# Decoder layer in one kernel: three feed-forward products moved ahead of the stage change, and the down projection's additions and requests re-timed

## What is computed

```
def finish(x, o_att, y_ssd, W):
    mix = concat([o_att, y_ssd])
    h = x + mix @ W['w_out']
    u = rmsnorm(h, W['norm_ffn'])
    return h + (silu(u @ W['w_gate']) * (u @ W['w_up'])) @ W['w_down']
```

## Time and profile before

| what | us |
|---|---|
| median of three runs | 1787.85 |
| profiled execution | 1803.71 |
| its span | 1801.9 |
| TensorE busy (94% of the span) | 1693.7 |
| VectorE busy (64%) | 1153.6 |
| ScalarE busy (42%) | 762.5 |
| GpSimd busy (23%) | 407.9 |

### The profile page before, as it was taken

The page is one execution under the profiler, slowest core; times in us unless marked ns, Lnnn a source line. Parts: engine busy times, 40 slices in busy tenths (PEclk is TensorE's granted clock), DMA queues, the critical chain, the costliest instruction groups (busy, mean ns, idle before and its releaser), DMA issues. The chain is left out here.

```text
span 1801.9 us, 32859 instructions
## 1 busy us (share of the span) xinstructions
PE 1693.7 (94%) x11957; PEld 1436.6 (80%) x11957; DVE 1153.6 (64%) x2521; ACT 762.5 (42%) x1593; POOL 407.9 (23%) x488
## 2 busy tenths in 40 slices
PE   5999998999999989998888996999999999999998
PEld 5999997888876756555546876999999999877777
DVE  7632257766675645565354368877788877597875
ACT  6322462777672335455343234323223232364432
POOL 1321120766664643344432001000000000000000
PEclk9999999899998989999988998999999999999999
DMA  5633111121001256556683231322223321684333
GB/s 160 103 108 109 36 42 25 28 48 26 19 12 36 82 208 217 164 193 236 211 298 132 73 100 56 112 88 94 88 94 115 114 88 65 235 289 125 86 112 104
DMA packets 161031, 204.19 MB, mean 113 GB/s; under 512 B 55110, under 2 KB 109423, under 8 KB 160850
## 3 DMA queue, kind: packets, MB, share of 16 engines
q1 hardware_dynamic: 142170, 135.00, 24.8%
q0 software_dynamic: 18432, 67.12, 11.1%
q10 hardware_dynamic: 312, 0.52, 0.1%
HBM read 164.69 MB, written 37.90 MB: 112 GB/s over the span
## 5 line engine op out<-in xcount | busy, mean ns | idle before, releaser
L2911 PE MATMUL banks<-u_sum,w_sum 128*128 128x264 f32 x3696 | 450.7, 284 | 9.7 <-DVE w_sum L2944 9.7
L2911 PEld LDWEIGHTS banks<-u_sum,w_sum 128*128 128x128 f32 x3696 | 450.4, 189 | 9.9 <-issue 9.8
L470 PE MATMUL banks<-u_parts_mix,w_in_parts 128*128 128x352 f32 x1440 | 243.6, 326 | 4.4 <-DVE u_parts_mix L837 4.4
L470 PEld LDWEIGHTS banks<-u_parts_mix,w_in_parts 128*128 128x128 f32 x1440 | 230.7, 189 | 7.8 <-DVE u_parts_mix L837 4.8
L1979 PE MATMUL banks<-turned,cmp_w 128*128 128x512 f32 x256 | 133.7, 605 | 5.0 <-DVE turned L2106 3.0
L2104 ACT ACTIVATE turned<-banks 128x512 f32<-128x512 f32 (+1 forms) x136 | 78.6, 587 | 138.5 <-PE banks L1967 105.1
L3240 PE MATMUL banks<-wd_hi,gd_hi 128*128 128x512 f32 x308 | 122.3, 397 | 9.6 <-DVE y_sums L3289 7.6
L3240 PE MATMUL banks<-wd_lo,gd_hi 128*128 128x512 f32 x308 | 121.9, 396 | 0.0
L3240 PE MATMUL banks<-wd_hi,gd_lo 128*128 128x512 f32 x308 | 121.7, 395 | 0.0
L1967 PEld LDWEIGHTS banks<-consts,rows_grouped 128*128 128x128 f32 x512 | 65.0, 144 | 68.7 <-issue 57.1
L2834 ACT ACTIVATE w_sum<-w_whole 128x512 fp32r<-128x512 f32 x110 | 66.6, 624 | 105.9 <-DVE w_whole L2938 105.9
(11 more groups left out here) (436 smaller groups left out, 3127.5 us busy)
## 6 DMA issues: line engine op xcount, KB each, us to landing
gd_whole<-g_sums SPq DMA_DIRECT2D x77, 256.0 KB, 2.7
g_sums<-silu_gate SPq DMA_DIRECT2D x55, 256.0 KB, 2.1
w_gate_raw<-in_w_gate SPq DMA_DIRECT2D x11, 1024.0 KB, 5.4
w_up_raw<-in_w_up SPq DMA_DIRECT2D x11, 1024.0 KB, 5.3
w<-in_w_down SPq DMA_DIRECT2D x44, 256.0 KB, 5.2
w_in_raw<-in_w_in SPq DMA_DIRECT2D x29, 256.0 KB, 3.4
g_sums<-s SPq DMA_DIRECT2D x22, 256.0 KB, 2.3
x_tile<-in_x_prompt SPq DMA_DIRECT2D x8, 512.0 KB, 4.2
```

What stands on the lines that cost most here:

```text
L470: mm = nc.tensor.matmul(bank[:, 0:PIECE], w[:, pb, :], u[:, pa, k, tokens(p)], start=(k == 0 and (pa, pb) == TERMS[0]), stop=(k == KT - 1 ...
L2911: mm = nc.tensor.matmul(bank(tg, i), wp[side, p][:, a, k, :], m.u[tg, i, b][:, k, :], start=(k == 0 and (a, b) == TERMS[0]), stop=(k == kh ...
```

## The change

1. Gate products 1, 3 and 5 of the first pair and token group 0 (`FIRST`) are computed in `stage_finish_mixer`, between the transposes of tiles 7 and 8, into banks 6, 7 and 2. Their weight sums and splits are made by VectorE and ScalarE behind the splits of tile 6, ahead of tile 7's addition. The splits of token products 4 and 2 (two of the seven) move from tile 6 to tile 5.
2. Group 1's token sums 4 and 7 are made by GpSimd (`EARLY_POOL`) and sums 1 and 3 by VectorE (`EARLY_DVE`) at the end of the mixer; 7, 1 and 3 only for 232 of 264 columns. The missing 32 columns (tile 8) and sum 6 are done by VectorE in the feed-forward stage, which no longer uses GpSimd.
3. `stage_ffn` starts with product 4. Four more small writes (memset) raise the semaphores for the work already done. The pair loop of TensorE has its first pair written out. Banks are renumbered in both stages (0 with 6, 1 with 7).
4. In the down projection the additions come in front of step 3 of each of the last four products (before: 4, 5, 5, 5), and SyncE asks for one entry of `later` per step until step 15, then for two.

```diff
+                pe.wait_ge(s.h_ready, 2 * NT)
+                for p, i in enumerate(FIRST):
+                    pe.wait_ge(m.first_split, p + 1)
+                    pe.wait_ge(s.u_split, p + 1)
+                    for k in range(KT // 2):
+                        for a, b in TERMS:
+                            mm = nc.tensor.matmul(m.bank[FIRST_BANKS[i]][:, 0:QUARTER], m.first_wp[p][:, a, k, :], m.u[0, i, b][:, k, :],
...
+                    mm.then_inc(m.first_done, 1)
                 turn_h(n - 1)
...
+                pool.wait_ge(s.u_whole, 2 * (NT - 1))
+                pool.wait_ge(s.mixed, 2 * n)
+                early_sum(EARLY_POOL[0], slice(0, QUARTER))
+                pool.wait_ge(s.u_whole, 2 * NT)
+                pool.wait_ge(m.early_sum, 1)
+                early_sum(EARLY_POOL[1], slice(0, EARLY_COLS))
...
+                        if i == NT:
+                            early_sum(EARLY_DVE[0])
                         dve.wait_ge(s.h_root, i + 1)
...
+                        if i == NT:
+                            early_sum(EARLY_DVE[1])
...
-                        for p in {5: range(3), 6: range(3, 7)}.get(i, ()):
+                        for p in {5: range(5), 6: range(5, 7)}.get(i, ()):
...
+                        for p in {NT - 2: range(len(FIRST))}.get(i, ()):
+                            dve.wait_ge(m.gate_in, 16)
...
-POOL_SUMS = 3
+FIRST, FIRST_BANKS = PRODUCTS[:3], {1: 6, 3: 7, 5: 2}
+EARLY_POOL, EARLY_DVE, EARLY_COLS = (4, 7), (1, 3), NT * P - 3 * QUARTER
...
-D_ADDED_AT = {3: 2, 2: 3, 4: 4, 1: 5, 6: 5, 7: 5}
+D_ADDED_AT = {3: 2, 2: 3, 4: 3, 1: 3, 6: 3, 7: 3}
...
-                            plans = ([ul[:1], [us[0], ul[1]], [us[1], ul[2]], ul[3:4], ul[4:5]],
+                            plans = ([first[:2], first[2:] + us[:2] + ul[:1], [ul[1], us[2], us[3], ul[2]], ul[3:4], ul[4:5]],
...
-                for f in weights((None, 0), 0):
-                    f()
+                dve.wait_ge(m.first_done, len(FIRST))
...
+                first = [lambda f=f, p=p: f((None, 0), 0, p) for f, p in
+                         ((w_sum, 4), (w_lo, 3), (w_sum, 5), (w_sum, 6), (w_lo, 4), (w_lo, 5), (w_lo, 6))]
...
-        later += [top[q], w(0, 1, 2 * q), w(0, 1, 2 * q + 1)]
-    later += [w(0, 1, p) for p in range(8, PAIRS)] + bottom
+        later += [top[q], w(0, 1, q)]
+    later += [w(0, 1, p) for p in range(4, PAIRS)] + bottom
...
-        for what in later[:2]:
+        count = 1 if j < G_SLOTS + PAIRS - 1 else 2
+        for what in later[:count]:
             one_of(what)
-        later = later[2:]
+        later = later[count:]
```

More of the change, by code:

```diff
@@ L2441, in stage_finish_mixer @@
     m.gate_raw = nc.alloc_sbuf_tensor_at("w_gate_raw", [P, KT, 2 * P], F32, offset=m.mix_start + size)
-    m.gate_raw_end = m.mix_start + size + KT * 2 * P * 4
+    first = Region(nc, m.mix_start + size + KT * 2 * P * 4, m.end)
+    m.first_whole, m.first_wp = {}, {}
+    for p in range(len(FIRST)):
+        m.first_whole[p] = nc.alloc_sbuf_tensor_at(f"w_whole_first_{p}", [P, KT // 2, P], F32, offset=first.at + KT // 2 * P * 4)
+        m.first_wp[p] = first(f"w_sum_first_{p}", [P, 2, KT // 2, P], F32R)
+    m.first_end = first.at
     low = Region(nc, m.base_end + 17 * size, m.mix_start)
@@ L2578, in _, with early_sum @@
             def _(pool):
+                def early_sum(i, cols):
+                    _, a, b, op = next(u for u in U_SUMS if u[0] == i)
+                    nc.gpsimd.tensor_tensor(m.u_whole[1, i][:, :, cols], m.u_whole[1, a][:, :, cols], m.u_whole[1, b][:, :, cols],
+                                            op).then_inc(m.early_sum, 1)
                 for k in SPLIT_BY_POOL:
@@ L2714, in stage_ffn @@
     mid = Region(nc, m.u1_end, m.mix_start)
-    top = Region(nc, m.gate_raw_end, m.end)
+    top = Region(nc, m.first_end, m.end)
     up_raw = top("w_up_raw", [P, KT, 2 * P])
@@ L2755, in over_pairs @@
         turn((None, last), False)
[L2757 removed]
+    with stage(nc, "landed*2 w_sum w_hi w_split u_sum u_hi u_split m_done copied c_done silu_done g_ready "
                    "t_sum plain_stored s5_stored first_stored second_stored "
@@ L2856, in first_gate @@
                     u_hi(1)
-                    copy(t, 0, 0, 5)
-                    u_hi(2)
-                    u_hi(3)
                     copy(t, 0, 0, 2)
-                    for p in range(4, 7):
+                    for p in range(2, 7):
                         u_hi(p)
@@ L2891, in turn @@
                                 silu(t, tg)
-                for p in range(7):
+                act.wait_ge(m.early_sum, len(EARLY_POOL))
+                act.wait_ge(m.early_sum_dve, len(EARLY_DVE))
+                hi((None, 0), 0, 3)
+                copy((None, 0), 0, 0, 5)
+                for p in range(4, 7):
                     hi((None, 0), 0, p)
@@ L2914, in turn @@
                                 mm.then_inc(s.m_done, 1)
-                with pe.Fori(0, last) as t:
-                    turn(t)
-                turn(last)
+                turn((None, 0))
+                with pe.Fori(0, last - 1) as t:
+                    turn((t, 1))
+                turn((None, last))
                 down_tensor(nc, pe, s, d)
-            @block.gpsimd
-            def _(pool):
-                for k in range(POOL_SUMS):
-                    i, a, b, op = U_SUMS[k]
-                    nc.gpsimd.tensor_tensor(m.u_whole[1, i][:, :, :], m.u_whole[1, a][:, :, :], m.u_whole[1, b][:, :, :],
-                                            op).then_inc(s.u_sum_pool, 1)
             @block.vector
```

72 lines of the change are left out of this document (54 added, 18 removed).

## The result

The changed kernel takes **1777.56 us** (median of 6 runs, 1776.73 to 1780.38) beside 1787.83 of the kernel before in the same comparison (6 runs, 1785.83 to 1788.24): ratio 0.9947, 95% interval 0.9937 to 0.9957. The forecast was 1774, range 1768 to 1780.5. The time lies in the range; of the 14.0 us forecast 10.3 came.

A forecast was written before the change was run, and what follows sets the result against it. TensorE, busy for 94% of the span, was taken as the bound. Stage change 8.7 us plus down projection 5.3 (13.6 freed, 8.3 lost) made 14.0 off 1787.85: 1774 us, range 1768 to 1780.5.

The forecast's parts named there:

- Early matmuls and split weights in the mixer, cost 0: Mixer's end: 36 matmuls fit TensorE's 4.6 us idle before tile 8's transposes; the added work costs 0, at worst 1 us.
- Turn-taking at the mixer's end: Two-input SBUF steps of VectorE and GpSimd alternate, holding sum 1; the new stage begins 1.5 us later, 0.4 without this.
- the case that I named through the Trainium skill: Mixer's end: tile 8's scaling also waits if GpSimd's sum 7 ends after 1089.5; forecast had it ending at 1088.4.
- Stage change 8.7 us: Gate to up products: TensorE starts up at 1113.9, later weights cost some 0.5 more, against 1123.1 before; 8.7 us gained.
- Late additions, 5.2 + 3.3 us: Last products of the down projection: earlier additions remove 5.2 us of `y_sums` waits and 3.3 us of half speed.
- Opening, 5.1 us: Start of the down projection: one request per step lands blocks sooner, saving 1.0 + 2.4 and 1.7 of half speed.
- the forecast's own sign: Down projection: waits standing at its first two products would show the forecast wrong in that term.
- `rest_h` too late, 8.3 us: Down projection, step 27: `rest_h` is requested only after step 26; 6.5 us idle and 1.8 of half speed lost.
- `rest_h` in time: Rival: the request for `rest_h` causes no wait in the down projection; gain 22.3 us, 1765.6 us; chance 0.08.
- late weight blocks: Rival: in product 3 of the down projection nine steps wait some 2.5 us each; net 8 us slower, 1796; chance 0.04.
- the stage change gave more than half: Answers the rival that the stage change gives half: 4 us less gained, 1778 us; chance 0.08.
- of the opening's loss a quarter stayed: Answers the rival that the down projection's opening stays as it is: 5.1 us missing, 1779 us; chance 0.17.

The follow-up runs named there:

- products_behind: The changed kernel with the 36 early matmuls behind tile 8's transposes instead of ahead of them; 1802.7 us, ratio 0.9985 to the kernel before.
- down_only: The kernel before with only the changed kernel's down projection edits (addition table and request list); 1804.4 us, ratio 0.9998 to the kernel before.
- rest_two_steps: The changed kernel with the request for the last rows of h at step 30 instead of 32; 1783.1 us, ratio 0.9873 to the kernel before.
- gate_only: The changed kernel with the additions and request list of the kernel before, leaving only mixer and gate changes; 1796.0 us, ratio 0.9943 to the kernel before.
- stores_later: The changed kernel with product 3's four stores issued behind step 33's requests instead of step 31's; 1794.8 us, ratio 0.9930 to the kernel before.

## Why the prediction was right, and where it was off

Each term of the sum was found at the place where the forecast had it. That the terms, as traced, add up to the timed gain is in part luck, as the end of this section says.

- **Early matmuls and split weights in the mixer, cost 0: right.** From tile 6's to tile 7's transposes it is 12.0 us before and after. products_behind showed that their place is worth more than I had given it.
- **Turn-taking at the mixer's end: the mechanism right, the held step another.** I had sum 1 held to over 2 us and the new stage 1.5 us later. Its 3.26 us and VectorE's timeline show that GpSimd's second sum gave way to sum 1 and ended late, and that tile 8's scaling then waited behind it. I had GpSimd 0.5 us ahead with sum 7; in the trace the two began 0.13 us apart, so which step was held hung on tenths. That is the case that I named through the Trainium skill (page "SBUF — State Buffer", section "Who interferes with whom": a `tensor_scalar` can be held too) and then set aside, since I had sum 7 end in time. The trace agrees: 1.88 us beside sum 7, 0.74 without it. The stage began 1.1 us later, not 1.5.
- **Stage change 8.7 us: right, 8.56 against the trace of before, 7.7 against that of down_only.** The first up product came at 1113.8 on the clock of before's trace, forecast 1113.9 and 0.5 behind. The half speed behind the 3.06 us wait was absorbed: VectorE was the pace. In rest_two_steps it lasted 5.4 us in place of 3.3, and the first up product still came 30.1 us behind the mark. gate_only gives 8.55.
- **Late additions, 5.2 + 3.3 us: the waits right, the half speed a matter of chance.** All five waits went. Of six waits of 1.7 to 1.8 us in three traces three were followed by half speed, so the fair price was 5.2 and some 1.7.
- **Opening, 5.1 us: 3.7 came.** The wait in step 7 and the half speed went; of 2.40 us 1.35 was left in the changed kernel's trace (0 to 1.35 over the nine executions whose list starts the same). By the forecast's own sign, a wait left at the first two products, this term was wrong; what sets the rest of the wait stays open. Its 2.1 and 3.9 MB also leave out the load `rest`, 0.35 MB.
- **`rest_h` too late, 8.3 us: it is the step that failed in size, 10.6.** Place, cause and order of events came as forecast. The term used landing times from a quiet queue, but four stores of 256 KB issued just ahead filled the DMA engines (share 1.03 over the 2 us from the block's request, 0.52 in stores_later): 0.8 us in the block's request, 0.8 in the landing. Without them it was 6.83. (The forecast's own terms for this wait add up to 6.4, not 6.5.) Half speed behind it cost 2.0 us, in place of 1.8.

Together the terms make 8.6 + 5.2 + 3.3 + 3.7 - 10.6 = 10.2 us, and 10.8 was traced, 10.3 timed. They are read against one execution of the kernel before, which had its long half speed at the stage change and both stretches in the last products; with 7.7 and 1.7 for these two the sum is 7.7. The timed gain lies, by its interval, between 7.7 and 11.3 us. The rivals: `rest_h` in time is refuted; so are late weight blocks, since no wait in the trace ends with one; the stage change gave more than half; of the opening's loss a quarter stayed.

## What to carry to other kernels

When a list of requests is thinned out, work out for its last entry when it is now issued and when it is needed; here the last entry took back 10.6 of the 12.2 us that the same edit and its neighbour gave, and moving it by two steps brings nearly all of it. Price a landing behind whatever the same queue has issued just ahead, stores included. Independent matmuls put in a gap can be worth more than their duration: here 4.6 us of them cost 6.2 when they stood behind the gap, 2.3 of it through half speed.

## What the runs showed of the hardware

- Half speed behind a short stop is not certain, and neither is its length. In the down projection it came behind three of six waits of 1.69 to 1.81 us, behind three of three of 2.40 to 2.45, and behind none of 1.23 or less. Behind the same 3.06 us at the stage change it lasted 3.3 us from TensorE's restart in the changed kernel (to 1081.7) and 5.4 in rest_two_steps (to 1100.8); at the old stage change, behind 9.70 and 9.98 us, it lasted 5.2 and 3.1. The rows are of the changed kernel and of rest_two_steps, with all five busy shares:

```profile
1079.00:1080.00 1.00, 1.00 (x7) 1.00 (x6) 1.00 (x3) 0.32 (x1) 0.00 (x0) 0.50 1.07 381
1081.00:1082.00 1.00, 1.00 (x7) 1.00 (x7) 1.00 (x3) 0.00 (x0) 0.00 (x0) 0.64 0.23 74
```

```profile
1098.00:1099.00 1.00, 1.00 (x6) 1.00 (x6) 1.00 (x3) 0.00 (x0) 0.00 (x0) 0.50 0.25 79
1100.00:1101.00 1.00, 1.00 (x7) 1.00 (x7) 0.61 (x1) 1.00 (x2) 0.00 (x0) 0.61 0.60 118
```

- The kernel before takes 1787.8 us in the comparison of the result and 1803 to 1807 on the three chips of the experiments. In the changed kernel's two traces, 18 us apart, the difference lies ahead of the mark, and the 460 us behind it agree within 0.1 us. A fixed mark in both traces told tenths that no median did, where the clock behind it did not differ.
- GpSimd's second sum began at 1070.82 by its row and VectorE's sum 1 at 1070.95, and yet VectorE's ran through in 1.10 us and GpSimd's took 3.26. Starts 0.1 us apart don't tell who goes first, and with the order of two such steps the held step moves down the chain.
